# Taking the first pair of experts out of the loop, with the running sum turned behind its first products

## The reference

```python
x = _layernorm(DEEPNORM_ALPHA * x + mix, ln1_g, ln1_b)
ffn = _moe(x.reshape(n_b * s_len, d), router_w, router_b, moe_w_gu, moe_b_gu, moe_w_down, moe_b_down)
x = _layernorm(DEEPNORM_ALPHA * x + ffn.reshape(n_b, s_len, d), ln2_g, ln2_b)
...
logits = jnp.dot(x2d.astype(f32), router_w.astype(f32)) + router_b.astype(f32)
top_val, top_idx = lax.top_k(logits, TOP_K)
top_w = jax.nn.softmax(top_val, axis=-1)
...
hgu = xb @ moe_w_gu[e] + moe_b_gu[e]              # 1024 x 2048 per expert
gate = jnp.minimum(hgu[:, :D_EXPERT], SWIGLU_LIMIT)
up = jnp.clip(hgu[:, D_EXPERT:], -SWIGLU_LIMIT, SWIGLU_LIMIT)
act = (up + 1.0) * gate * jax.nn.sigmoid(SWIGLU_ALPHA * gate)
return act @ moe_w_down[e] + moe_b_down[e]        # 1024 x 1024 per expert
```

## Time and profile before

| | us |
|---|---|
| median of 3 runs | 1287.73 |
| lowest and highest of them | 1283.1, 1288.95 |
| profiled execution, its time | 1286.78 |
| its span | 1284.8 |
| PE busy, share of the span | 90% |
| DVE, ACT, POOL busy | 30%, 24%, 2% |
| granted clock of PE, mean | 0.983 |
| moved by DMA | 456.68 MB |

### The profile page before, as it was taken

The page is one execution under the profiler, slowest core; times in us unless marked ns, Lnnn a source line. Parts: engine busy times, 40 slices in busy tenths (PEclk is TensorE's granted clock), DMA queues, the critical chain, the costliest instruction groups (busy, mean ns, idle before and its releaser), DMA issues.

```text
span 1284.8 us, 18179 instructions
## 1 busy us (share of the span) xinstructions
PE 1152.7 (90%) x7008; PEld 611.2 (48%) x7008; DVE 388.6 (30%) x715; ACT 310.4 (24%) x536; POOL 19.5 (2%) x42
## 2 busy tenths in 40 slices
PE   6999999987999999989888998989898989888895
PEld 5998878985344343333333333433333333333341
DVE  4788477755203202020202021120202020202025
ACT  5685444336220211202020202111120202020101
POOL 1000020000000000000000000000000000000000
PEclk9999999995999999999999999999999999999998
DMA  9645576861999999999999999999999999999992
GB/s 292 206 125 175 161 247 220 309 238 62 395 418 418 419 417 419 417 418 419 417 417 417 417 417 417 418 419 418 418 418 418 418 419 418 418 417 417 415 416 94
DMA packets 118100, 456.68 MB, mean 355 GB/s; under 512 B 10344, under 2 KB 49272, under 8 KB 84944
## 3 DMA queue, kind: packets, MB, share of 16 engines
q1 hardware_dynamic: 113984, 445.52, 87.3%
q0 software_dynamic: 2864, 10.26, 2.5%
q10 hardware_dynamic: 1216, 0.42, 0.1%
HBM read 450.21 MB, written 5.95 MB: 355 GB/s over the span
## 4 chain that ended last, share of the span: by engine, by line
PE 44%; DMA 26%; SPq 19%; DVE 5%; issue 4%; ACT 2%; DVEq 0%; ACTq 0%
DMA gu_w<-in_moe_w_gu 25%; PE pool L538 16%; PE pool L808 11%; SPq L381 10%; SPq L386 9%; PE pool L841 7%; PE ob L820 3%; PE ub L820 2%; PE ub L772 1%; PE ub L760 1%; ACT arena L1077 1%; PE pool L834 1%; PE pool L547 1%; ACT wh L874 1%; DVE wl L1115 1%
## 5 line engine op out<-in xcount | busy, mean ns | idle before, releaser
L808 PE MATMUL pool<-gu_w,arena 128*64 128x512 f32 x2048 | 468.4, 600 | 42.2 <-DMA gu_w<-in_moe_w_gu 41.9
L808 PEld LDWEIGHTS pool<-gu_w,arena 128*64 128x64 f32 x2048 | 140.7, 137 | 352.1 <-issue 213.3
L1532 DVE TENSOR_SCALAR arena<-pool 128x512 f32<-128x512 f32 x32 | 22.1, 692 | 756.3 <-PE pool L808 756.3
L841 PE MATMUL pool<-dn_w,arena 128*64 128x512 f32 x1024 | 226.8, 595 | 21.6 <-ACT arena L1077 21.6
L538 PE MATMUL pool<-xh,wh 128*128 128x264 f32 x576 | 167.3, 290 | 6.4 <-DVE xl_most L1108 5.5
L538 PE MATMUL pool<-xh,wl 128*128 128x264 f32 x576 | 164.3, 285 | 0.0
L841 PEld LDWEIGHTS pool<-dn_w,arena 128*64 128x64 f32 x1024 | 70.7, 137 | 157.1 <-issue 127.9
L538 PE MATMUL pool<-xl_most,wh 128*128 128x264 f32 x504 | 144.2, 286 | 0.0
L1075 ACT ACTIVATE arena<-arena 128x512 f32<-128x512 f32 x32 | 20.2, 630 | 485.4 <-DVE arena L1532 485.4
L538 PEld LDWEIGHTS pool<-xh,wh 128*128 128x128 f32 x576 | 109.9, 191 | 13.0 <-issue 10.3
L538 PEld LDWEIGHTS pool<-xh,wl 128*128 128x128 f32 x576 | 109.5, 190 | 0.0
(11 more groups left out here) (285 smaller groups left out, 723.4 us busy)
## 6 DMA issues: line engine op xcount, KB each, us to landing
gu_w<-in_moe_w_gu SPq DMA_DIRECT2D x256, 1024.0 KB, 19.9
dn_w<-in_moe_w_down SPq DMA_DIRECT2D x256, 512.0 KB, 20.2
dn_w<-in_w_in SPq DMA_DIRECT2D x24, 1024.0 KB, 5.4
dn_w<-in_w_branch SPq DMA_DIRECT2D x8, 1024.0 KB, 6.3
gu_w<-in_state_gla POOLq DMA_DIRECT2D x8, 512.0 KB, 7.0
out_gla_sample<-gu_w POOLq DMA_DIRECT2D x8, 512.0 KB, 5.1
dn_w<-in_w_o SPq DMA_DIRECT2D x4, 1024.0 KB, 6.7
arena<-in_xT SPq DMA_DIRECT2D x2, 1056.0 KB, 7.1
```

Of the source, the lines that this page charges most:

```text
L808: last = mm(out, xg[:, k, j * CAP:(j + 1) * CAP], gu_w[:, k, cols], start=False, stop=(k == NB - 1))
L841: last = mm(DOWN[s * CAP:(s + 1) * CAP, :], act_t[:, k % 4, k // 4 * CAP:(k // 4 + 1) * CAP], dn_w[:, k, s * HF:(s + 1) * HF], start=(k == ...
```

## The change

The first pair of experts is taken out of the loop, as a call of `body` of its own with `first=True`, on PE, DVE and ACT; SP's loop still covers all pairs. On PE, `turn_x` no longer stands on both sides of `rk`. It stands behind the products on `gu_w` of expert 0, goes through banks of PSUM of its own list (`xt_banks`), and PE goes on only when ACT has read all eight blocks (`xt_read`). ACT's `running_sum` stands behind its first sigmoid. Where the first three blocks stood, `keep_clock(11)` runs 11 matrix products whose result nobody reads. The gather of the first pair is split: the first half stands ahead of the bias products of expert 0, the second half between rows 3 and 4 of `gu_w`. Its takes are signalled block by block (`xg0_act`, `xg0_dve`), and the products on row `k` wait only for block `k`. The split of the tokens writes to `xrest`, since `ytok` must last until `turn_x`; the buffers `gbuf` to `sbuf_` and `act_s` move for the same reason.

```diff
-    jobs += ["lg"] + [f"xt{n}" for n in range(3)] + ["rk"] + [f"xt{n}" for n in range(3, NB)]
+    jobs += ["lg", "rk"]
...
-        gbuf, ubuf, tbuf, sbuf_ = (slot(8, i * HF, HF) for i in range(4))
-        act_s = slot(9, 0, HF)
+        gbuf, ubuf, tbuf, sbuf_ = (slot(7, i * HF, HF) for i in range(4))
+        xrest = slot(5, 0, NT * D).rearrange("p (t n) -> p t n", t=NT)
...
+        act_s = Sg[:, 0:2, :].rearrange("p h v -> p (h v)")
...
+            with eng.Fori(first, PAIRS - 1) as pair:
...
-            def turn_x(blocks_):
-
-                for n in blocks_:
-                    name = f"xt{n}"
-                    turn(name, [(bank(name)[:, first:first + rows], ytok[0:rows, t, n * P:(n + 1) * P])
-                                for t, (first, rows) in enumerate(TILES)])
+            def keep_clock(count):
+
+                for i in range(count):
+                    mm(ub[:, 1, 0:T], yT[:, i % NB, 0:P], yT[:, i % NB, :], start=True, stop=True)
...
-            pe.wait_ge(y_norm, NT)
-            turn_x(range(3))
+            keep_clock(11)
...
-            turn_x(range(3, NB))
+            pe.wait_ge(y_norm, NT)
             pe.wait_ge(pick0_done, 1)
-            for half in range(2):
+
+            def gather_first(half):
+
                 for t, (first, rows) in ((2, TILES[2]), (0, TILES[0]), (1, TILES[1])):
                     for c in range(4):
                         n = 4 * half + c
                         last = mm(GATH[:, half, c * P:(c + 1) * P], ytok[0:rows, t, n * P:(n + 1) * P], pick0[0:rows, t, :],
                                   start=(t == 2 and c == 0), stop=(t == 1), skip_group_check=True)
                 last.then_inc(gath0, 1)
-            pe.wait_ge(gath0, 2)
-            pe.sem_inc(gath_done, 1)
+
+            xt_banks = [ob[:, 0, :], ob[:, 1, :], ub[:, 0, :], ub[:, 1, :], DOWN, ACTT, ob[:, 0, :], ob[:, 1, :]]
+
+            def turn_x():
+
+                for n in range(NB):
+                    if n >= 6:
+                        pe.wait_ge(xt_read, n - 5)
+                    for t, (first, rows) in enumerate(TILES):
+                        last = nc.tensor.transpose(xt_banks[n][:, first:first + rows], ytok[0:rows, t, n * P:(n + 1) * P],
+                                                   ident[0:rows, 0:rows])
+                    last.then_inc(xt_full, 1)
+                pe.wait_ge(xt_read, NB)
...
-            for n in range(4, NB):
-                wait_drained(pe, f"xt{n}")
-            pe.wait_ge(xg0_dve, 1)
+            gather_first(0)
+            for name in ("yt11", "yt21", "lg", "rk"):
+                wait_drained(pe, name)
...
+                    if j == 0 and not first:
+                        pe.wait_ge(xg_ready, it)
...
+                        if first and j == 0:
+                            if k == 4:
+                                gather_first(1)
+                            pe.wait_ge((xg0_act, xg0_dve)[k // 4], k % 4 + 1)
...
+                    if first and j == 0:
+                        turn_x()
...
-            body(moe_loops(pe, body), PAIRS - 1, final=True)
+            body(0, 0, first=True)
+            body(moe_loops(pe, body, 1), PAIRS - 1, final=True)
...
-            for n in range(NB):
-                wait_filled(sc, f"xt{n}")
-                a(yacc[:, n, :], bank(f"xt{n}")[:, 0:T], ACT.Identity, bias=affine[:, NB + n:NB + n + 1],
-                  scale=affine[:, n:n + 1]).then_inc(dr(f"xt{n}"), 1)
+            xt_banks = [ob[:, 0, :], ob[:, 1, :], ub[:, 0, :], ub[:, 1, :], DOWN, ACTT, ob[:, 0, :], ob[:, 1, :]]
+
+            def running_sum():
+
+                for n in range(NB):
+                    sc.wait_ge(xt_full, n + 1)
+                    a(yacc[:, n, :], xt_banks[n][:, 0:T], ACT.Identity, bias=affine[:, NB + n:NB + n + 1],
+                      scale=affine[:, n:n + 1]).then_inc(xt_read, 1)
...
-                last = take(n, GATH[:, 0, n * P:(n + 1) * P])
-            last.then_inc(xg_ready, 1)
+                take(n, GATH[:, 0, n * P:(n + 1) * P]).then_inc(xg0_act, 1)
...
+                    if first and j == 0:
+                        running_sum()
...
-                last = ts(xg[:, n, :], GATH[:, 1, n % 4 * P:(n % 4 + 1) * P], con("ln1_g")[:, n:n + 1], con("ln1_b")[:, n:n + 1],
-                          ALU.mult, ALU.add)
-                if n < NB - 1:
-                    me.done(last)
-            last.then_inc(xg0_dve, 1)
-
-            def part_left(part, made, left):
+                ts(xg[:, n, :], GATH[:, 1, n % 4 * P:(n % 4 + 1) * P], con("ln1_g")[:, n:n + 1], con("ln1_b")[:, n:n + 1],
+                   ALU.mult, ALU.add).then_inc(xg0_dve, 1)
...
+            def part_left(part, whole, made, left):
 
                 for t in (0, 1, 2):
                     rows = TILES[t][1]
                     v.wait_ge(made, t + 1)
-                    tt(ytok[0:rows, t, :], ytok[0:rows, t, :], xparts[t][part][0:rows, :], ALU.subtract).then_inc(left, 1)
-
-            part_left(0, xp_hi, xp_r1)
+                    tt(xrest[0:rows, t, :], whole[0:rows, t, :], xparts[t][part][0:rows, :], ALU.subtract).then_inc(left, 1)
+
+            part_left(0, ytok, xp_hi, xp_r1)
...
+            v.wait_ge(stored_early, 32)
...
+                            if not first:
+                                v.wait_ge(gath_done, it)
+                            choose(slice(2, 4) if first else bass.ds(it * 2 + 2, 2))
```

More of the change, by code:

```diff
@@ L301, in build @@
         y_stat, y_var, y_std, y_rs, y_norm = (sem(n) for n in ("y_stat", "y_var", "y_std", "y_rs", "y_norm"))
-        cdw_done, cd_read, pick0_done, gath0, xg0_dve = (
-            sem(n) for n in ("cdw_done", "cd_read", "pick0_done", "gath0", "xg0_dve"))
+        cdw_done, pick0_done, gath0, xg0_act, xg0_dve = (
+            sem(n) for n in ("cdw_done", "pick0_done", "gath0", "xg0_act", "xg0_dve"))
+        xt_full, xt_read = sem("xt_full"), sem("xt_read")
         lg_done, ex_done, sel_done, flag_done = (sem(n) for n in ("lg_done", "ex_done", "sel_done", "flag_done"))
@@ L359, in settle, with moe_loops @@
                 self.eng.wait_ge(self.s, self.base + self.n)
-        def moe_loops(eng, body):
-            with eng.Fori(0, PAIRS - 1) as pair:
+        def moe_loops(eng, body, first=0):
+            with eng.Fori(first, PAIRS - 1) as pair:
                 body(pair, pair)
@@ L792, in final_rows, with body @@
                        start=(c == 0), stop=False)
-            def body(it, pair, final=False):
+            def body(it, pair, final=False, first=False):
                 for j in range(2):
                     n = it * 2 + j
-                    if j == 0:
-                        pe.wait_ge(xg_ready, it + 1)
+                    if j == 0 and not first:
+                        pe.wait_ge(xg_ready, it)
                     pe.wait_ge(gu_read, n + 1)
@@ L1067, in _, with body @@
                     sc.wait_ge(ready, t + 1)
-                    nc.scalar.copy(xparts[t][part][0:rows, :], ytok[0:rows, t, :]).then_inc(made, 1)
+                    nc.scalar.copy(xparts[t][part][0:rows, :], xrest[0:rows, t, :]).then_inc(made, 1)
             nc.scalar.copy(rs[0:1, 0, 0:1], ident[0:1, 0:1]).then_inc(eo_ready, 1)
-            def body(it, pair, final=False):
+            def body(it, pair, final=False, first=False):
                 for j in range(2):
@@ L1078, in body @@
                     if j == 1 and not final:
-                        sc.wait_ge(gath_done, it + 2)
+                        sc.wait_ge(gath_done, it + 1)
                         for b in range(NB):
@@ L1091, in body @@
                     last.then_inc(eo_ready, 1)
-            body(moe_loops(sc, body), PAIRS - 1, final=True)
+            body(0, 0, first=True)
+            body(moe_loops(sc, body, 1), PAIRS - 1, final=True)
             for i, t in enumerate((2, 0, 1)):
@@ L1523, in _, with body @@
             V.tensor_copy(wpick[:, :, 0:E], wtx[:, :, 0:E]).then_inc(wpicked, 1)
-            part_left(1, xp_mid, xp_r2)
+            part_left(1, xrest, xp_mid, xp_r2)
+            v.wait_ge(stored_early, 32)
             ts(flag[:, :], red[:, 0, 0:1], float(CAP), None, ALU.is_gt).then_inc(flag_done, 1)
-            def body(it, pair, final=False):
+            def body(it, pair, final=False, first=False):
                 me.n, me.base = 0, it * STEP + base
@@ L1534, in body @@
                     if not (final and j == 1):
-                        one_hot(slice(e + 1, e + 2) if final else bass.ds(e + 1, 1))
+                        one_hot(slice(e + 1, e + 2) if final or first else bass.ds(e + 1, 1))
                     if j == 0:
@@ L1551, in body @@
                             tt(y, y, (SCAT, SCAT2)[d % 2][:, :, 0:T], ALU.add).then_inc(scat_read, 1)
-                        own = slice(E - 2, E) if final else bass.ds(pair * 2, 2)
+                        own = slice(E - 2, E) if final else slice(0, 2) if first else bass.ds(pair * 2, 2)
```

(3 more changed lines are left out.)

2 lines of the change are left out of this document (removed).

## The result

The changed kernel takes **1292.1 us** (median of 15 runs, 1290.06 to 1297.85); the kernel before took 1287.55 us in the same comparison (15 runs, 1282.77 to 1289.36). The medians lie 4.5 us apart. The ratio, estimated from all the runs, is 1.0054, 95% interval 1.0041 to 1.0066: half a per cent slower, 7.0 us by it (the two medians alone give 1.0035). The profiled execution of the changed kernel took 1296.97 us (span 1295.0), 10.2 us more than that of before; it is the third slowest of its 15 runs. Three stretches make up the 10.2 us. In the rows, `<-issue` stands for idle time in which the engine waited for nothing that the profile shows.

The account below looks back on a forecast made before the run. The prediction took DMA to bound the experts and the end to follow expert 0's down products. Starting these 2.9 us earlier gave 1286.78 - 2.9 = 1283.9 us profiled, 1284.8 us as median; range 1280 to 1290 us (8 in 10).

Parts of the forecast that it names:

- What bounds the kernel: Whole run: experts are bound by DMA, 30.1 us each; the end follows when DMA starts running without a break.
- The end follows the start of expert 0's down products: First pair: the down products, at 338.63 us before, set the end; forecast 335.7 us, 2.9 us earlier.
- From there on everything issued is the same as before: Behind expert 0's down products: nothing issued differs, so no further term enters the sum.
- Rival 3: Loop entry: PE stalls on the branch near 369 us under saturated DMA; 1290 us and more, chance 0.04.
- Ranks and `pick0`: Before the gather: without transposes, L1469 comes at 296.0 us in place of 298.24, `pick0` at 297.0 us.
- First half of the gather: Expert 0: 24 records at full clock take 2.9 us, bias 0.6; first products at 300.6 us, 15.7 us earlier.
- rival 1: Gather of the first pair: clock falls before it, costing 4.7 us; slower, 1289.5 us, chance 0.24.
- The rule that the prediction takes from the Trainium skill: Clock: transposes are not counted as busy like other matmuls, so `turn_x` loses the clock but the first gather would hold it.
- What is late next: DVE and ACT: takes, split and table load last 12.0 us, now outlasting the products; 12.7 of 15.7 us gone.
- Running sum: Behind ACT's first sigmoid: eight uncovered scalings at 0.5 us each, 4.0 us; turned weights copied at 327.8 us.
- Scatter to down: From DVE's copy to the down products: 5.66 us, plus 2.2 us for the scatter at 1.2 GHz.
- The sum for the first pair: Down products of expert 0 at 335.7 us in place of 338.63, 2.9 us earlier.

Follow-up runs that it names:

- experiments 1 to 6: Follow-up kernels; without own line: 3, the kernel before with 44 tiny products at PE's start, ratio 1.0004; 6, experiment 4 with three more fillers before the gather, 1282.55 us.
- experiment 1: Changed kernel with four tiny products (16 instructions) ahead of the first projection, moving the code behind the loop; 1289.17 us, ratio 1.0012.
- experiment 4: Experiment 1 with DVE making the first part of the split and the routing weights before the takes of the gather's second half; 1285.19 us, ratio 0.9985.
- experiments 1 and 5: 5: changed kernel without its 11 fillers, code behind the loop placed as in experiment 1; 1289.19 us, ratio 1.0018. Experiment 1 has its own line.
- experiment 7: Experiment 4 with the running sum and scatter moved behind the second expert's products on PE, DVE and ACT; 1287.54 us, ratio 1.0006.
- experiment 2: Kernel before with 34 tiny products (136 instructions) at PE's start, code behind the loop 14 instructions ahead of a multiple of 256; 1291.67 us, ratio 1.0049.

## Why the prediction was wrong, step by step

**What bounds the kernel: right for the loop, wrong for its end.** "The end follows the start of expert 0's down products" held through the whole loop: the distance from them to the exit is 867.47 us before and 866.6 to 867.6 in the changed kernel and experiments 1 to 6. The sentence behind it, "From there on everything issued is the same as before", is **the step that failed**. It took the work for the time. Behind the loop PE is the bound, its code had moved, and that cost 6.5 us: 22.46 us from the exit to the turned weights in place of 15.98. Rival 3 had the right mechanism, a stall on a branch under saturated DMA, and the right row, and looked only at the loop's entry. There no stall showed: the bias products at 375.79 us follow without idle time. The position of the code behind the loop, which any edit shifts that adds or removes instructions of PE ahead of it, was in no term of the sum.

**Ranks and `pick0`: right.** The forecast was M + 9.7 for `pick0`; DVE made it from 300.60 to 301.16 us, M + 9.6, and the gather began at M + 9.7.

**First half of the gather: mis-sized, by rival 1.** It took 4.29 us and not 2.9, the bias 1.03 and not 0.6, since the clock fell to 0.50 in the gather, behind the 1.40 us in which PE waited; from 306 us it came back, so that of rival 1's 4.7 us only 1.9 came. The same wait stood ahead of the gather in experiment 1, and there the clock stayed: the forecast of 2.9 was right in kind for that run, and which of the two comes is not decided by anything found here. The second half took 3.13 us against 2.9. DVE's takes stood at M + 24.9 in place of M + 23.2. The rule that the prediction takes from the Trainium skill (TensorE: Matmul & The Clock Gate, Part 4: PE-mode transpose) speaks of transposes. The gather is ordinary products, and in the row from 304 us it ran at 0.50 all the same, as the earlier trace rows had it; so that rule does not keep it safe.

**What is late next: right.** From the takes to the end of the table load it is 316.53 to 328.56 us, 12.03 us against 12.0. Experiment 4 confirms the chain by breaking it.

**Running sum: right.** Scalings follow each other every 0.46 us (forecast 0.5).

**Scatter to down: right in kind, 0.6 us more.** At the low clock, as forecast, from DVE's copy 333.88 to 342.37, 8.5 us against 7.9; the turned weights too were at the low clock, 0.3 more.

**The sum for the first pair** was 2.9 us gained and is 0.6: 1.7 lost at the gather and its takes, 0.3 and 0.6 at the turned weights and the scatter, and 0.2 back from the scalings. With the 6.5 us of the exit it makes 5.9 us slower, between the 4.5 us of the medians and the 7.0 us of the ratio. The 4.3 us of the mixer in the profiled run are left out of it.

**The base of that sum is a second weak step.** The 2.9 us were subtracted from one profile of before, M + 51.35, in which gather and first products ran at the low clock for longer than in the two later ones (M + 46.9 and M + 47.1). Against those, the forecast 335.7 us, M + 48.4, would itself have been a loss of more than 1 us. How often the kernel before runs one way or the other is not known from three profiles, so the good agreement of 5.9 us is partly luck. What the times say of the change without its second pause: experiments 1 and 5 have medians 2.3 us above the kernel before, ratios 1.0012 and 1.0018, no gain in either.

**Open.** Which step of the mixer decides between its early and its late end was not tried. How far ahead of the multiple of 256 the second pause begins is known at three distances only: there at 4 and 14 instructions, absent at 150 (and absent at 12 and 26 past it). Whether it needs DMA at a share of 1.02 was not tried either. What the change by itself does to the first pair, at equal clocks, is open within some 4 us.

## What to carry to other kernels

The branch out of this loop, under saturated DMA, had a price that depended on where its target lay in the list of instructions, and any edit ahead of it that adds or removes instructions moves that target: before an edit of a per cent or less is judged, compare the pauses at the loop's exit in both profiles, and shift the code by a few cheap instructions to tell position from work. Take the start of a forecast from more than one profile where the clock changes in the stretch: here the same stretch of the kernel before took 46.9 to 51.35 us. An early start is worth what the next engine in line lets through; here the order of two groups on DVE decided more than the 14 us won ahead of it. And a queue of transfers in order wants a steady supply, not only an early first consumer: experiment 7 started the down products 8 us sooner after M than experiment 4 and lost more than that behind them.

## What the hardware showed that was not expected

**A second pause behind a taken branch.** PE stood 3.3 to 3.7 us at every exit of the loop, and 5.09 or 2.82 us again in the two kernels whose code there began 4 or 14 instructions ahead of a multiple of 256. The Trainium skill, Runtime: NRT & Kernel Launch, Instruction fetch mechanics, describes blocks of 256 instructions fetched by DMA one ahead, with a taken branch out of the window waiting for its block, and calls the crossing of a block "mostly hidden". The traces agree with the wait at the branch; close behind it, with the DMA engines at a share of 1.00 to 1.02, the crossing was not hidden: 5.09 us beside the branch's 3.46 in the changed kernel, 2.82 beside 3.34 in experiment 2. That it is a fetch is this reading of the page; the runs show the position and the price.

**The same code runs at two clocks.** The mixer, the same code but for the tiny products at its start, ended between 286.11 and 293.38 us in nine profiles; from 260 to 280 us its granted clock was 0.83 in the changed kernel, 0.91 before and 1.00 in experiment 2, though that the clock alone makes the difference is not shown. The gather of the kernel before took 8.70 to 11.47 us in three, and the first half of the changed kernel's gather took 3.11 us in two profiles and 4.29 to 4.32 in three with the same products ahead of it but for three fillers. With differences of that size from run to run, single profiles place a stall but do not size a gain of 1 or 2 us.
